# Modulation vector by fused sums on VectorE, output-projection tiles between the last attention units, two low parts moved to VectorE

## The reference, cut to what matters

```python
def second_block(x, c, ada_w, ada_b, ...):
    mod = jax.nn.silu(c) @ ada_w[l] + ada_b[l]           # (1, 1024) @ (1024, 6144)
    sh1, sc1, g1, sh2, sc2, g2 = jnp.split(mod, 6, axis=-1)
    h = modulate(rms_norm_2(x, pre_norm_mix[l]), sh1, sc1)
    y = hybrid_mixer(h, ...)                              # ends in concat(norm(rnn), norm(att)) @ w_out
    x = x + (1.0 + g1) * rms_norm_2(y, post_norm_mix[l])
    h = modulate(rms_norm_2(x, pre_norm_mlp[l]), sh2, sc2)
    y = jnp.square(jax.nn.relu(h @ w_ff1[l])) @ w_ff2[l]
    return x + (1.0 + g2) * rms_norm_2(y, post_norm_mlp[l])
```

## Time and profile before

| | us |
|---|---|
| median of 3 runs | 1754.05 (1753.17 to 1755.69) |
| the profiled execution | 1754.21 |
| its span in the trace | 1752.2 |
| TensorE (PE) busy | 1732.2 |
| VectorE (DVE) busy | 1290.2 |
| ScalarE (ACT) busy | 769.0 |
| GpSimd (POOL) busy | 23.2 |

### The profile page before, as it was taken

How to read it: one execution, slowest core, us unless ns; L and a number is a source line. 1 busy time by engine, 2 the same in 40 slices (tenths; PEclk the granted TensorE clock), 3 DMA queues, 4 the chain that set the end, 5 groups by cost and what they waited for, 6 DMA issues and landing times.

```text
span 1752.2 us, 23118 instructions
## 1 busy us (share of the span) xinstructions
PE 1732.2 (99%) x8700; PEld 1407.9 (80%) x8700; DVE 1290.2 (74%) x1882; ACT 769.0 (44%) x1053; POOL 23.2 (1%) x9
## 2 busy tenths in 40 slices
PE   9999999999999999999999999999999999999998
PEld 8896888888888989688888888788766788888886
DVE  6368786887787645878688688757589468777778
ACT  6324442333333523344233233345798365454442
POOL 0000000000000000000000000000000400000000
PEclk9999999999999999999999999999999999999999
DMA  7330334334333233043433433363410222322331
GB/s 277 121 120 25 126 115 144 120 120 138 125 120 120 97 106 111 30 151 107 138 117 119 142 120 120 120 173 121 121 37 2 72 97 100 117 97 97 106 111 49
DMA packets 33209, 194.76 MB, mean 111 GB/s; under 512 B 5744, under 2 KB 7152, under 8 KB 11120
## 3 DMA queue, kind: packets, MB, share of 16 engines
q1 hardware_dynamic: 24656, 156.77, 26.1%
q10 hardware_dynamic: 8480, 36.97, 6.7%
HBM read 186.91 MB, written 2.11 MB: 108 GB/s over the span
## 4 chain that ended last, share of the span: by engine, by line
PE 91%; DVE 4%; issue 2%; DMA 1%; ACT 1%; POOL 0%; SPq 0%; DVEq 0%; ACTq 0%; PEldq 0%
PE ps L578 28%; PE ps L580 28%; PE ps L579 28%; PE ps L728 1%; PE ps L742 1%; PE ps L1002 1%; PE ps L1018 1%; PE ps L984 1%; DMA raw<-in_weights 1%; DVE acc L2626 1%; DMA both<-in_weights 0%; PE ps L750 0%; DVE pb L2413 0%; PE ps L915 0%; DVE wl L1891 0%
## 5 line engine op out<-in xcount | busy, mean ns | idle before, releaser
L578 PE MATMUL ps<-xh,wh 128*128 128x512 f32 x1440 | 567.4, 394 | 4.7 <-DVE xl L1850 2.5
L580 PE MATMUL ps<-xh,wl 128*128 128x512 f32 x1440 | 561.6, 390 | 0.0
L579 PE MATMUL ps<-xl,wh 128*128 128x512 f32 x1440 | 561.1, 390 | 0.0
L1174 ACT ACTIVATE wh<-raw 128x2048 fp32r<-128x2048 f32 x128 | 244.6, 1913 | 279.6 <-DMA raw<-in_weights 276.0
L578 PEld LDWEIGHTS ps<-xh,wh 128*128 128x128 f32 x1440 | 270.6, 188 | 64.6 <-issue 7.4
L580 PEld LDWEIGHTS ps<-xh,wl 128*128 128x128 f32 x1440 | 270.4, 188 | 56.8
L579 PEld LDWEIGHTS ps<-xl,wh 128*128 128x128 f32 x1440 | 270.6, 188 | 56.1 <-issue 1.4
L1891 DVE TENSOR_TENSOR wl<-raw,wh 128x2048 fp32r<-128x2048 f32 x108 | 247.0, 2287 | 90.4 <-ACT wh L1174 90.3
L1401 ACT ACTIVATE cv<-upb,prm 128x512 f32<-128x512 f32 x88 | 67.0, 809 | 253.1 <-DVE upb L2091 253.1
L578 PE MATMUL ps<-wh,xh 128*128 128x256 f32 (+1 forms) x352 | 108.0, 307 | 0.2 <-POOL wl L560 0.2
L579 PE MATMUL ps<-wl,xh 128*128 128x256 f32 (+1 forms) x352 | 106.6, 303 | 0.0
(11 more groups left out here) (326 smaller groups left out, 2572.5 us busy)
## 6 DMA issues: line engine op xcount, KB each, us to landing
raw<-in_weights SPq DMA_DIRECT2D x129, 1024.0 KB, 4.9
adab<-in_ada ACTq DMA_DIRECT2D x22, 1024.0 KB, 4.9
both<-in_weights SPq DMA_DIRECT2D x7, 2048.0 KB, 7.7
t<-in_cst ACTq DMA_DIRECT2D x1, 3200.0 KB, 10.3
x<-in_xin SPq DMA_DIRECT2D x8, 256.0 KB, 6.0
turned<-q ACTq DMA_DIRECT2D x8, 256.0 KB, 4.2
turned<-k ACTq DMA_DIRECT2D x8, 256.0 KB, 4.5
adab_tail<-in_ada ACTq DMA_DIRECT2D x2, 1024.0 KB, 12.7
```

The lines of the kernel that those rows point to most:

```text
L578: pe.matmul(out, w_hi, m_hi, start=start, stop=False)
L579: pe.matmul(out, w_hi, m_lo, start=False, stop=False)
L580: return pe.matmul(out, w_lo, m_hi, start=False, stop=stop)
L1174: act.activation(wh[:, s, :], raw[:, s, :], ACT.Copy).then_inc(hi_made, 1)
```

## The change

**Modulation.** The slab of `ada_w` is laid out the other way round: output channels on the partitions, all 1024 input channels along the row. `c`, repeated on 128 partitions (`crow`, 512 KB), is loaded once, and ScalarE takes its Silu in place where it took that of the 8 columns before. A piece is then two instructions on VectorE that multiply 1024 elements with `crow` and add them up (`ada_sum`), and a copy of the two columns into `mod` (`ada_keep`). TensorE has no part in it: `ada_part` and all its waits on `ada_evac` are gone.

**Attention's end.** Tile 2 of `WO2` moves ahead of `turn(26)`, tile 3 ahead of `turn(27)`, tile 0 ahead of `values(27)`; tile 1 stays last.

**Low parts.** Those of `WO2 + 1` and `WO2 + 2` are made by VectorE in `attention_norm`, behind the scaling of x and ahead of the last addition of squares; GpSimd keeps `WO2`, `FF0 - 1` and `FF0`.

```diff
@@ gpsimd
             low(OWN, OWN % RING)
             pool.wait_ge(sq_added, SQ_RNN + 6)
-            for n in range(OWN + 1, FF0):
-                low(n, n % RING)
+            low(FF0 - 1, (FF0 - 1) % RING)
             pool.wait_ge(nt4_ready, 8)
             low(FF0, FF0 % RING)
@@ tensor
-            def ada_part(a):
-
-                past(pe, ada_summed, a + 1)
-                past(pe, ada_evac, a)
-                for m in range(2):
-                    last = pe.transpose(ps[:, 7, m * P:(m + 1) * P], ada_acc[:, m * P:(m + 1) * P], ident)
-                last.then_inc(ada_done, 1)
-
...
                         down(it * 2 + v, v, n + 2, (MLP0 + 4) % RING)
-                        ada_part(j + l * NG)
...
-                if U == UNITS - 1:
+                if U == UNITS - 2:
                     pe.wait_ge(rnn_low, 4)
                     pe.wait_ge(*split(WO2))
                     pe.wait_ge(sc_done, unit_signals(UNITS - 2))
                     out_tokens(WO2, 0, 2, (0, 1, 2, 3), True, False)
+                if U == UNITS - 1:
+                    out_tokens(WO2, 0, 3, (0, 1, 2, 3), True, False)
                 turn(U)
                 if U:
                     values(U - 1)
-            out_tokens(WO2, 0, 3, (0, 1, 2, 3), True, False)
+            pe.wait_ge(sc_done, unit_signals(UNITS - 1))
+            out_tokens(WO2, 0, 0, (0, 1, 2, 3), True, False)
             values(UNITS - 1)
-            pe.wait_ge(sc_done, unit_signals(UNITS - 1))
-            for i in range(2):
-                last = out_tokens(WO2, 0, i, (0, 1, 2, 3), True, False)
-            last.then_inc(slab_used, 1)
+            out_tokens(WO2, 0, 1, (0, 1, 2, 3), True, False).then_inc(slab_used, 1)
@@ scalar
+            act.dma_start(crow[:, :], crow_in).then_inc(crow_loaded, 16)
...
-                        act.activation(silu_c[:, :], col(PC_C, KT), ACT.Silu).then_inc(silu_c_ready, 1)
+                        act.wait_ge(crow_loaded, 16)
+                        act.activation(crow[:, :], crow[:, :], ACT.Silu).then_inc(crow_ready, 1)
@@ vector
             def ada_sum(a, buf, loaded):
 
                 dve.wait_ge(ada_loaded, loaded * 16)
-                past(dve, ada_done, a)
-                for kt in range(KT):
-                    if kt == 0:
-                        ins = dve.tensor_scalar(ada_acc[:, :], buf[:, 0, :], silu_c[:, 0:1], None, ALU.mult)
-                    else:
-                        dve.wait_ge(ada_term, a * (KT - 1) + kt)
-                        ins = dve.scalar_tensor_tensor(ada_acc[:, :], buf[:, kt, :], silu_c[:, kt:kt + 1], ada_acc[:, :],
-                                                       ALU.mult, ALU.add)
-                    ins.then_inc(ada_term if kt < KT - 1 else ada_summed, 1)
-
-            def ada_out(a):
-                past(dve, ada_done, a + 1)
-                dve.tensor_reduce(cols(mod, a * 2, 2), ps[:, 7, 0:GRP].rearrange("p (m k) -> p m k", m=2), AX.X, ALU.add).then_inc(ada_evac, 1)
+                past(dve, ada_kept, a)
+                for m in range(2):
+                    ins = dve.tensor_tensor_reduce(out=buf[:, m, :], in0=buf[:, m, :], in1=crow[:, :], scale=1.0, scalar=0.0,
+                                                   op0=ALU.mult, op1=ALU.add, accum_out=ada_pair[:, m:m + 1])
+                ins.then_inc(ada_summed, 1)
+
+            def ada_keep(a):
+
+                past(dve, ada_summed, a + 1)
+                dve.tensor_scalar(cols(mod, a * 2, 2), ada_pair[:, :], 1.0, None, ALU.mult).then_inc(ada_kept, 1)
...
                     dve.tensor_scalar(x[:, b, :], x[:, b, :], inv_tok[:, 6, b % NT:b % NT + 1], None, ALU.mult).then_inc(x2_ready, 1)
+                for n in (OWN + 1, OWN + 2):
+                    low_slab(n, n % RING, mid_split)
                 add_four(3, sqb2, (3,))
```

More of the change, by code:

```diff
@@ L69 @@
 PC_FINAL = PC_CONV + LAYERS * PC_CONVN
-PC_C = PC_FINAL + 8
-PC_ADAB = PC_C + 8
+PC_ADAB = PC_FINAL + 8
 PC_PREMIX = PC_ADAB + 48
@@ L190, in build @@
         lru_c = keep("lru_c", [P, 6, 4])
-        ada_acc = keep("ada_acc", [P, GRP])
+        ada_pair = keep("ada_pair", [P, 2])
         tn = keep("tn", [P, 4, 8])
@@ L236, in build @@
         yt = at("yt", [P, KT, S], F32, arena)
-        adab = at("adab", [P, 8, GRP], F32, va_at + 8192)
-        assert mix_end <= 229368, mix_end
+        adab = at("adab", [P, 2, D], F32, va_at + 8192)
+        crow_at = 225248
+        crow = at("crow", [P, D], F32, crow_at)
+        assert mix_end <= crow_at, mix_end
         top[0] = arena
@@ L282, in build @@
         kkl = at("kkl", [P, 2, KKW], F32R, big + 24576 + size([P, 2, KKW]))
-        assert big + 24576 + 2 * size([P, 2, KKW]) <= 229368, big
+        assert big + 24576 + 2 * size([P, 2, KKW]) <= crow_at, big
         att = at("att", [P, 4, S], F32, big)
@@ L319, in build @@
         slab_split = sem("slab_split")
-        late_split = sem("late_split")
+        late_split, mid_split = sem("late_split"), sem("mid_split")
         first_loaded = [sem(f"first_loaded{kt}") for kt in range(KT)]
@@ L329, in build @@
         constants_set = sem("constants_set")
-        silu_c_ready = sem("silu_c_ready")
+        crow_loaded, crow_ready = sem("crow_loaded"), sem("crow_ready")
         lru_exp = sem("lru_exp")
@@ L572, in _ @@
             pe.sem_inc(slab_used, RING)
-            for s in tensor_counts:
-                pe.sem_inc(s, 1)
             def product(out, w_hi, w_lo, m_hi, m_lo, start, stop):
@@ L585, in split @@
                     return slab_split, n + 1
-                if isinstance(n, int) and n <= FF0:
-                    return late_split, n + (1 - OWN)
-                return late_split, n - OWN
+                if isinstance(n, int) and OWN < n < FF0 - 1:
+                    return mid_split, n - OWN
+                return late_split, n - OWN - 1 if n > OWN else 1
             def slab_fm(n, s, b0, fresh=None, half=None, kts=tuple(range(KT)), start=True, stop=True, first=False, free=None, ready=None,
@@ L817, in down @@
                             past(pe, ffn_added, l * 8 * NG + j * 8)
-                        if wide and o == 3:
-                            past(pe, ada_evac, NG)
                         if o >= (6 if wide else 3):
@@ L853, in _ @@
                     for kt in (0, 1, 2, 3, 7, 6, 4, 5):
-                        if t == 0 and kt == 7:
-                            past(pe, ada_evac, LAYERS * NG)
                         if t == 0 and kt >= 4:
@@ L912, in recurrent_gates @@
                         pe.wait_ge(cmp_kept, 1)
-                    elif which == 1:
-                        past(pe, ada_evac, ADA_SLABS)
                     pe.matmul(bank(gate_bank(which, i)), lru[:, which, i, :], cx[:, i, :], start=True, stop=True).then_inc(lru_ready, 1)
@@ L2066, in _ @@
                 square_sum(1)
-                dve.wait_ge(silu_c_ready, 1)
+                dve.wait_ge(crow_ready, 1)
                 ada_sum(l * NG, adab, l * NG + 1)
@@ L2148, in _ @@
                     gate_low(0, 0, r)
-                ada_out(l * NG)
+                ada_keep(l * NG)
                 if l == 1:
@@ L2178, in _ @@
                         add_down(it * 2 + v, n + 2, values_part, early=(6, 7))
-                        ada_out(l * NG + j)
+                        ada_keep(l * NG + j)
                 def weighted(t):
@@ L2223, in _ @@
             guard(3)
-            past(dve, ada_evac, LAYERS * NG)
+            past(dve, ada_kept, LAYERS * NG)
             def fold(n, scale, g):
@@ L2249, in _ @@
             dve.memset(kkl[:, :, :].bitcast(F32), 0.0).then_inc(zeroed, 1)
-            ada_out(LAYERS * NG)
+            ada_keep(LAYERS * NG)
             low2(4)
@@ L2282, in _ @@
             low2(6)
-            ada_out(LAYERS * NG + 1)
-            past(dve, ada_evac, ADA_SLABS)
+            ada_keep(LAYERS * NG + 1)
+            past(dve, ada_kept, ADA_SLABS)
             biased(40, 8)
@@ L2747 @@
     assert n == SLABS
-    ada = np.stack([slab8(a["ada_w_2"][0][:, i * GRP:(i + 1) * GRP]) for i in range(ADA_SLABS)])
+    ada = a["ada_w_2"][0].T.reshape(ADA_SLABS, 2, P, D).transpose(0, 2, 1, 3).reshape(ADA_SLABS, P, SLABW)
     prm = []
@@ L2756 @@
         prm.append(taps.transpose(4, 2, 1, 3, 0).reshape(P, PC_CONVN))
-    prm += [columns(a["final_g"]), columns(a["c_2"][0]), columns(a["ada_b_2"][0])]
+    prm += [columns(a["final_g"]), columns(a["ada_b_2"][0])]
     prm += [columns(a[m][0]) for m in ("pre_norm_mix_2", "post_norm_mix_2", "pre_norm_mlp_2", "post_norm_mlp_2")]
@@ L2782 @@
         "ada": ada,
+        "crow": np.broadcast_to(a["c_2"], (P, D)),
         "params": prm,
```

24 lines of the change are left out of this document (8 added, 16 removed).

## The result

The kernel after takes 1743.56 us (median of 4, 1743.38 to 1743.87), the kernel before in the same job 1753.61 (1752.94 to 1755.69): ratio 0.9941, 95% interval 0.9927 to 0.9956. It is faster, by 10.05 us where 6.05 were forecast, and so outside the range (1745.0 to 1750.8). The direction was right and a size was wrong, so the question is where 4 us more come from.

A forecast was written before the change was run, and what follows sets the result against it. TensorE was taken to bound the kernel (91% of the chain). Modulation 4.8 + 0.3 = 5.1 us and attention 0.95 us make 6.05 off 1754.21, so 1748.2, and 1748.0 for the median; range 1745.0 to 1750.8.

The forecast's parts named there:

- The transposes: TensorE, 24 modulation pieces: removing a pair saves 0.22 us by distance of starts; 22 pairs counted, 4.8 us.
- the term of 5.1: Modulation's gain on TensorE: 4.8 us for 22 pairs plus 0.3 at the first; bounds 3 and 13.1 us.
- a transpose takes its busy time: Rival: each of 48 removed transposes saves its full 0.272 us on TensorE, so 1740 us; chance 0.06.
- not given back: Rival: TensorE arrives 0.22 us earlier but finds banks and low parts late; 1752.8 us if everywhere; chance 0.06.
- Behind the first piece: First modulation piece: TensorE's 0.53 us wait for a low part stays but ends 0.27 earlier; gain 0.3 us.
- The end of layer 1: Last pair of layer 1: TensorE's 1.31 us wait for a VectorE addition does not end earlier; gain 0.
- Sums, load of c: VectorE's piece falls from 3.9 to 2.6 us, worth 0; loading c early also 0, upper bound 1.5 us.
- The slack of 1.0 us: In `down`, output 0's addition ends 1.0 us before output 3 starts, so up to 4.9 us a piece costs nothing.
- the slow sum: Rival: VectorE's fused instruction delays `down`'s additions above 4.9 us a piece; 1796 us at three times; chance 0.04.
- Attention: End of the attention on TensorE: 0.84 + 0.21 - 0.1 = 0.95 us gained; bounds -0.5 and 1.1.
- the tiles: Attention's end: a reordered tile fills TensorE's 0.84 us wait at unit 26; one extra run of tiles loses 0.1.
- The low part was forecast at 0.21: Attention's end: making low parts on VectorE removes TensorE's 0.21 us wait for `WO2 + 1`.

The follow-up runs named there:

- after with 32 bytes: The kernel after with one unused tile of 32 bytes a partition ahead of the arena: 1745.83 us.
- kernel with three products: The kernel after with each fused product and sum on VectorE made three times over: 1843.17 us.
- the sum made twice: The kernel after with each fused product and sum on VectorE made two times: 1759.11 us.

## Why the prediction was half right

- **What bounds the kernel:** right. All of the gain is time between TensorE's starts.
- **The transposes:** right. 0.22 us a pair by the earlier trace rows, 0.24 measured for 20 pairs put back, and some 5.4 us for the stretches to which the term of 5.1 belongs (0.15 of it from the shorter sum, see below). The rivals "a transpose takes its busy time" (13.1 us for 48) and "not given back" are both refuted.
- **Behind the first piece:** forecast 0.3. The profiles show 0.65, but kernels built on before vary here by 0.1 to 0.4 with their start; the mean difference between the two families is 0.25. The low part now starts 0.07 us behind `ada_keep`, the distance that was assumed.
- **The end of layer 1:** near enough. From the matmul at 1137.46 to that at 1140.44 before, and from 1129.39 to 1132.37 after, there are 2.98 us: the wait of 1.31 stayed, and the one ahead of it grew from 0.16 to 0.44. The shift is 8.12 just ahead of the last pair and 8.07 behind both waits (after with 32 bytes: 5.92 and 5.93), so the last pair was worth nothing, as forecast.
- **Sums, load of c:** nearly right. A piece takes 2.3 us. The shorter sum was put at 0 and is worth 0.15, in the one step of the loop that had no slack. The load of c can't be told from the chance in the start. The slack of 1.0 us was read in one step and is not that of the loop; it cost the forecast little, but it put the edge of the slow sum at 4.9 us instead of about 4.15.
- **Attention:** the tiles were forecast at 0.84 - 0.1 = 0.74 and measured 0.81. The low part was forecast at 0.21, and is worth 0.46. The earlier trace rows shows 0.21 as idle time, which counts from the modelled end of the matmul ahead and not from where the next one could have started; the distance of starts from line 1060 to the fourth matmul of `WO2 + 1` was 2.04 us before (1369.63 to 1371.67) and is 1.55 after (1360.46 to 1362.01). This term was mis-sized, by the same habit that was avoided for the transposes.
- **The step that failed** is the total: "5.1 + 0.95 = 6.05 us off the profiled execution's 1754.21". It takes every matmul that the change does not touch as equally long in both kernels. Placement gave 2.3 us by the whole runs (after against after with 32 bytes) and 2.1 by the traces (layer 1; the 0.41 in the last product are lost again behind it), and the moved instruction fetch 0.84. The modulation's 5.4 are 0.25 for the first piece, 2.1 for the rest of layer 0, 2.8 for layer 1 (the shift in after with 32 bytes, where placement has no part) and 0.3 for the last two. With 1.3 for the attention all this makes 9.6 to 9.8; measured are 10.05. Without placement and fetch, 6.7 us would stand against the forecast 6.05, and the time (some 1747, an estimate from these sums) would lie in the range.

## What to carry to other kernels

When an edit adds or removes a tile, list the addresses of the matmuls' operands before and after, and compare the distance of starts in a long run of matmuls that nobody edited. Here 64 unused bytes were worth 5.0 us on top of a change worth 10. Cost a wait as a difference of starts over the whole place, not as the idle time that the row prints, and look at the granted clock of the matmuls behind it.

## What the runs showed of the hardware that was not expected

- With 128x512 matmuls back to back (both operands of type float32r), the step depends on where the two operands begin in SBUF relative to each other: 0.2266, 0.229 or 0.232 to 0.234 us, 3% between best and worst.
- Behind a wait of some 3 us TensorE runs at half clock (0.50 granted, 1.2 GHz) for mostly about 3.4 us, 1.5 us lost. The kernel with three products has 20 such waits in its loop, printed as 2.6 to 3.5 us; 19 are followed by 2.7 to 6.2 us of steps of 0.43 us, and one (2.59 us, at 908.17) by none. In the loop with the sum made twice, with printed waits of 0.1 to 0.65 us, the clock stayed at 1.00, and so it did behind the wait of 1.31 us.
- A fetch of 16 KB of TensorE's instructions that falls into a 2 MB load goes with a landing 1.1 us later (five kernels against fifteen), and moving TensorE's list by 12 or 20 instructions switches it.
- Without its six warm-up matmuls the kernel before took 1753.67 us in one run, no other than with them (1753.83), although its wait of 0.65 us at the second feed-forward net was gone.
